# Encoder layer on one core: two of the last eight output slices scaled and stored by GpSimd, one by VectorE, six stores left to SyncE

## Chip, cores, metric

The kernel is one launch on one core of one Trainium2 chip. The metric is device time in microseconds (us), the median of three runs. The profile is of one further execution of the same program; its times count from the start of its span.

## What is computed

One encoder layer (windowed attention, a long convolution, a gated merge, a squared-ReLU MLP) runs over two groups of tokens with shared weights: 512 tokens ("sample") and 256 tokens ("prompt"). What the change touches is the very last step, the final modulated RMSNorm of the residual stream:

```
shf, scf = jnp.split(c_act @ w_ada_final + b_ada_final, 2, axis=-1)
return modulate(rmsnorm(x, final_g), shf, scf)
# rmsnorm: y = x * rsqrt(mean(x*x) + eps) * g       modulate: y * (1 + scale) + shift
```

Everything is float32, D_MODEL is 1024.

## The kernel before

The activations lie transposed in on-chip memory: 128 partitions hold the features of one of eight slices (`KD = 8`), the columns are the 768 tokens, 512 of the sample group (half 0) and 256 of the prompt group (half 1). The program is written engine by engine, each engine's instructions in the order in which its block issues them, with semaphores between engines; nothing is scheduled by a planner.

At the end of the MLP, TensorE makes the last down projection for the sixteen (half, slice) pairs in the order of `PART_ORDER`, all of half 0 first. For each, VectorE adds the result to the residual stream `xT` (`residual_group`, L2198), ScalarE squares it (L1306), and TensorE sums the squares over the partitions. When half 0 is complete its scale 1/rms is spread over a PSUM tile `wk`, and its eight slices are normalised, scaled and stored between the steps of half 1: VectorE writes `y = xT * wk` (`t_half`, L1798), ScalarE applies the per-feature scale and shift (`y_half` of the scalar block, L1344), SyncE stores the slice (L598).

Half 1, 256 tokens, comes after the last matmul and is all that is left then. After its 1/rms (ScalarE L1725, VectorE L1770, TensorE L824) VectorE runs `t_half(2, 1, k)` for k = 0 to 7. Slices 2 and 5 (`Y_DVE`) are also scaled and shifted by VectorE itself (`y_half` of the vector block, L1807), each behind the `t_half` of the next slice; slices 0, 1, 3, 4, 6, 7 by ScalarE. SyncE stores all eight in the order 0 to 7 (L607), each behind the semaphore of its producer (`y_act`, `y_dve`), and then waits until all sixteen stores have landed (`stored`). A slice of half 1 is 128 x 256 float32, 128 KB.

GpSimd works on this kernel's early parts: additions of the convolution (L644, L683 to L713) and loads of weights from its own DMA queue (L634, L732, L740). Its last instruction in the program is the last load at L740.

Of the kernel before, what the change touches and what calls it, by code (L numbers as in the profile page):

```python
# [17 lines left out]
ALU = mybir.AluOpType  # L18
# [4 lines left out]
KD = D // P  # L23
# [32 lines left out]
SH1, SC1, G1, SH2, SC2, G2, SHF, SCF = (8 * i for i in range(8))  # L56
# [34 lines left out]


PART_ORDER = [(h, m) for h in range(2) for m in range(KD)]
Y_DVE = (2, 5)


LATE_DOT = [len([n for n in range(DOTS_OUT) if n % 3 == s]) for s in range(2)]
# [9 lines left out]
def program(nc, a, out_T):  # L107
    with ExitStack() as ctx:
        def sem(name):
            return ctx.enter_context(nc.semaphore(name))  # L110

        def region(*layouts):

            def size(layout):
                total = 0
                for _, shape, _ in layout:
                    n = 1
                    for d in shape[1:]:
                        n *= d
                    total += n  # L120
                return total

            assert max(map(size, layouts)) == size(layouts[-1])
            got = []
            for layout in layouts[:-1]:
                with ExitStack() as e:
                    got.append([e.enter_context(nc.sbuf_tensor(*t)) for t in layout])
            got.append([ctx.enter_context(nc.sbuf_tensor(*t)) for t in layouts[-1]])
            return got


        def sb(name, shape, dt=F32):
            return ctx.enter_context(nc.sbuf_tensor(name, shape, dt))
# [3 lines left out]
        wlo = [sb(f"w_lo{i}", [P, KD, P], F32R) for i in range(2)]  # L137

        (sqA, accA, _, mraw_c, _, crow, mrow), (wA,), (act,) = region(
            [("n0_sq", [P, 2, T], F32), ("n0_acc", [P, T], F32), ("act_gap", [P, 3 * T], F32), ("mod_raw_c", [P, 2, 512], F32),  # L140
             ("act_gap2", [P, 8 * T - P - 1024], F32), ("c_turned", [16, P], F32), ("mod_rows", [P, 2 * T], F32)],
            [("w_down_hilo", [P, 6, 2, KD, P], F32R)],
            [("act_hilo", [P, 2, KD, T], F32R)])

        ((hfA, fa, h1, zst, zh, fb, fk, ftab, dec, dec_p, ftab_p), (_, w3l),
         (_, cb3, junk3, _, ring3, s3f, c_st),
         (cos, sin, rt, vtmp, S0, PT0, S1, PT1, _, mask, _),
# [58 lines left out]
        modT = sb("modT", [P, 64, 2])  # L206
        asc = sb("norm_scale", [P, 3, KD, 2])
# [42 lines left out]
        f_stored = [sem(f"f_stored{i}") for i in range(4)]  # L250
        asc_done = sem("asc_done")
        m_sum, m_out, sqrt_set = sem("mod_sum"), sem("mod_out"), sem("sqrt_set")
        n_sq, n_acc, n_ps, n_std, n_rstd, n_spread, n_t, n_hf, n_hi, n_lo = (
            sem(n) for n in ("n_sq", "n_acc", "n_ps", "n_std", "n_rstd", "n_spread", "n_t", "n_hf", "n_hi", "n_lo"))
# [4 lines left out]
        fwd_ready, cross_step, prod_done = sem("fwd_ready"), sem("cross_step"), sem("prod_done")  # L259
        pc_copied, rot_done, pair_step = sem("pc_copied"), sem("rot_done"), sem("pair_step")  # L260
        tap_bias = sem("tap_bias")
        spec_first = m_sum
        inv_ready, inv_copied, y_done, z_done = (sem(n) for n in ("inv_ready", "inv_copied", "y_done", "z_done"))
        s_ready, s_max, s_neg, s_sd, s_es, s_exp, s_den, s_rden, s_norm = (
# [6 lines left out]
        y_act, y_dve, stored = (sem(n) for n in ("y_act", "y_dve", "stored"))  # L271
# [101 lines left out]
        def half(h):  # L373
            return slice(GROUPS[h][0], GROUPS[h][0] + GROUPS[h][1])

        def y_out(h, m):
            return out_T[:, m, half(h)]
# [90 lines left out]
        def _(sp):  # L468
# [128 lines left out]
                sp.wait_ge(y_act, m + 1)  # L597
                sp.dma_start(y_out(0, m), yT[:, m, half(0)]).then_inc(stored, 16)  # L598
            na = nd = 0
            for m in range(KD):  # L600
                if m in Y_DVE:
                    nd += 1
                    sp.wait_ge(y_dve, nd)
                else:
                    na += 1
                    sp.wait_ge(y_act, KD + na)
                sp.dma_start(y_out(1, m), yT[:, m, half(1)]).then_inc(stored, 16)  # L607
            sp.wait_ge(stored, 16 * 2 * KD)


        @block.gpsimd
        def _(pool):
# [125 lines left out]
            for n in range(KD, DOTS - DOTS_OUT):  # L738
                pool.wait_ge(dot_done, 2 * DOTS_OUT + 2 * n)
                pool.dma_start(ring3[:], w_adaT[n + DOTS_OUT]).then_inc(ld_dot[2], 16)  # L740

# [525 lines left out]
        def _(act_e):  # L1269
# [71 lines left out]
            def y_half(h, k):  # L1341

                act_e.wait_ge(n_t, 3 * KD + KD * h + k + 1)
                act_e.activation(yT[:, k, half(h)], yT[:, k, half(h)], ACT.Identity,  # L1344
                                 bias=modT[:, SHF + k, h:h + 1], scale=asc[:, 2, k, h:h + 1]).then_inc(y_act, 1)
# [146 lines left out]
            for t in range(T_MERGE):  # L1492
# [14 lines left out]
                elif t < T_GATE:  # L1507
                    m = t - T_HY
# [218 lines left out]
                if u >= KD:  # L1727
                    y_half(0, u - KD)
            for k in range(KD):
                if k not in Y_DVE:  # L1730
                    y_half(1, k)


# [1 line left out]
        def _(dve):  # L1735
# [53 lines left out]
            def t_half(q, h, k):  # L1789

                if k == 0:
                    dve.wait_ge(n_spread, 2 * q + h)
                if k == 1 and (q, h) != (2, 1):
                    dve.wait_ge(n_acc, KD + 16 * (q - 1) + KD * h + KD)
                if k >= 2 and q == 1:
                    dve.wait_ge(n_hf, KD + KD * h + k - 1)
                dst = yT[:, k, half(h)] if q == 2 else tnB[:, k % 2, half(h)]
                dve.tensor_tensor(dst, xT[:, k, half(h)], wk[:, half(h)], ALU.mult).then_inc(n_t, 1)  # L1798
# [5 lines left out]
            def y_half(k):  # L1804

                dve.wait_ge(n_t, 4 * KD + k + 1)
                dve.tensor_scalar(yT[:, k, half(1)], yT[:, k, half(1)], asc[:, 2, k, 1:2],  # L1807
                                  modT[:, SHF + k, 1:2], ALU.mult, ALU.add).then_inc(y_dve, 1)
# [716 lines left out]
            norm_rstd(2, 1)  # L2525
            for k in range(KD):
                t_half(2, 1, k)
                if k - 1 in Y_DVE:
                    y_half(k - 1)


def tables():
# [138 lines left out]
```

## Time and profile before

| | us |
|---|---|
| median of three runs | 1113.33 |
| lowest, highest | 1111.73, 1113.34 |
| the profiled execution, its own time | 1114.14 |
| its span | 1112.6 |

| engine | busy us | share of the span |
|---|---|---|
| TensorE (PE) | 1092.2 | 98% |
| TensorE weight loads (PEld) | 1022.2 | 92% |
| VectorE (DVE) | 802.3 | 72% |
| ScalarE (ACT) | 454.5 | 41% |
| GpSimd (POOL) | 108.9 | 10% |

The execution's own time is 1.5 us above its span: that much lies around what the profile shows. SyncE only issues DMAs, and such instructions are not counted as busy; a name with q (SPq, POOLq) is an engine's instruction queue. "TENSOR_TENSOR y<-xT,wk" reads: the instruction writes tile `y` from tiles `xT` and `wk`. A time to landing runs from the issue of a DMA to its completion.

### The profile page before, as it was taken

The page shows a single profiled execution, that of the slowest core. Times are in us where ns is not written, and L with a number is a line of the kernel's source. Part 1 is how long each engine was busy: PE and PEld are TensorE (multiplying, and loading weights), DVE is VectorE, ACT ScalarE, POOL GpSimd, SP SyncE. Part 2 cuts the span into 40 slices and gives each one's busy share as a digit, 9 for nine tenths or more (in the row PEclk, how much of TensorE's full clock was granted, in tenths as well). Part 3 has the DMA queues.
Part 4 walks back from the last instruction along what each step waited for, and adds up shares of the span by engine and source line. Part 5 has one row for each costly group of instructions (what it writes and reads, how often), then busy time and mean ns, then how long its engine had stood idle before and what let it go on. Part 6 is the DMA issues. An engine that isn't in the chain of part 4 may idle for free.

```text
span 1112.6 us, 16634 instructions
## 1 busy us (share of the span) xinstructions
PE 1092.2 (98%) x6304; PEld 1022.2 (92%) x6304; DVE 802.3 (72%) x1334; ACT 454.5 (41%) x792; POOL 108.9 (10%) x132
## 2 busy tenths in 40 slices
PE   6999999999999999999999999999999999999997
PEld 4787798888899999999899999999999999999886
DVE  5777699889388685556455777787978778788534
ACT  5631156665722322423246232253442526157414
POOL 2101200000334322000000000000000000000000
PEclk9999999999999999999999999999999999999998
DMA  9923454333332333753312331143333232222303
GB/s 345 394 86 117 154 189 143 129 127 114 119 123 105 119 104 124 282 153 108 110 57 95 125 121 57 57 152 99 111 103 106 95 109 91 87 76 76 95 19 115
DMA packets 45525, 138.85 MB, mean 125 GB/s; under 512 B 5051, under 2 KB 10635, under 8 KB 44556
## 3 DMA queue, kind: packets, MB, share of 16 engines
q1 hardware_dynamic: 29024, 80.21, 21.6%
q0 software_dynamic: 11376, 44.84, 11.3%
q10 hardware_dynamic: 5052, 12.81, 3.3%
q8 instruction: 47, 0.77, 0.3%
q14 instruction: 26, 0.21, 0.1%
HBM read 121.61 MB, written 15.74 MB: 123 GB/s over the span
## 4 chain that ended last, share of the span: by engine, by line
PE 93%; DVE 4%; DMA 1%; ACT 1%; issue 0%; ACTq 0%; DVEq 0%
PE acc_ps L750 39%; PE wk L1181 16%; PE acc_ps L1200 12%; PE acc_ps L832 12%; PE wk L1056 2%; PE acc_ps L839 1%; PE wk L991 1%; PE wk L980 1%; PE wk L970 1%; PE wk L1022 1%; PE wk L872 1%; PE wk L885 1%; DVE dot_out L1832 1%; DMA filt_zh<-in_t_z 1%; PE wk L803 1%; PE wk L890 1%
## 5 line engine op out<-in xcount | busy, mean ns | idle before, releaser
L750 PE MATMUL acc_ps<-act_hilo,w_hi 128*128 128x384 f32 x1504 | 332.5, 342 | 0.1
L750 PEld LDWEIGHTS acc_ps<-act_hilo,w_hi 128*128 128x128 f32 x1504 | 264.8, 189 | 18.8 <-issue 17.7
L750 PE MATMUL acc_ps<-act_hilo,w_lo 128*128 128x384 f32 x752 | 191.5, 335 | 0.0
L750 PEld LDWEIGHTS acc_ps<-act_hilo,w_lo 128*128 128x128 f32 x752 | 136.4, 188 | 0.0
L1200 PE MATMUL acc_ps<-hidden_hilo,act_hilo 128*128 128x384 f32 x768 | 134.6, 335 | 0.2
L1200 PEld LDWEIGHTS acc_ps<-hidden_hilo,act_hilo 128*128 128x128 f32 x768 | 133.2, 188 | 1.1 <-issue 1.1
L1741 DVE TENSOR_TENSOR w_lo<-w_raw,w_hi 128x1024 fp32r<-128x1024 f32 x61 | 76.3, 1252 | 55.1 <-ACT w_hi L1282 54.1
L1282 ACT ACTIVATE w_hi<-w_raw 128x1024 fp32r<-128x1024 f32 x61 | 64.2, 1053 | 44.3 <-PE acc_ps L750 40.9
L2198 DVE SCALAR_TENSOR_TENSOR xT<-acc_ps,modT,xT 128x512 f32<-128x512 f32 (+1 forms) x32 | 19.7, 617 | 59.7 <-PE acc_ps L832 59.5
L1832 DVE CUSTOM_DVE_ANT_0 dot_out<-dot_ring,c_rows,vecT 128x1024 f32<-128x1024 f32 x48 | 61.6, 1284 | 1.6 <-issue 0.6
L2323 DVE SCALAR_TENSOR_TENSOR xT<-acc_ps,modT,xT 128x384 f32<-128x384 f32 (+2 forms) x96 | 40.5, 478 | 28.8 <-PE acc_ps L1200 28.8
L750 PE MATMUL acc_ps<-hidden_hilo,w_hi 128*128 128x384 f32 x256 | 54.7, 334 | 0.0
L1515 ACT ACTIVATE gates_out<-acc_ps 128x768 f32<-128x768 f32 x16 | 13.0, 813 | 98.3 <-PE acc_ps L750 98.3
L832 PE MATMUL acc_ps<-hidden_hilo,w_down_hilo 128*128 128x512 f32 (+1 forms) x288 | 50.2, 336 | 0.0
L832 PEld LDWEIGHTS acc_ps<-hidden_hilo,w_down_hilo 128*128 128x128 f32 x288 | 44.4, 190 | 5.6
L1181 PE MATMUL wk<-act_hilo,w_hi 128*128 128x384 f32 x192 | 48.7, 334 | 0.0
L1181 PE MATMUL wk<-t_hilo,w_hi 128*128 128x384 f32 x192 | 48.7, 334 | 0.0
L2305 DVE TENSOR_TENSOR c_st<-wk,c_st 128x384 f32<-128x384 f32 x84 | 44.9, 551 | 2.7 <-PE wk L1181 2.3
L750 PEld LDWEIGHTS acc_ps<-hidden_hilo,w_hi 128*128 128x128 f32 x256 | 45.3, 188 | 0.0
L1614 ACT ACTIVATE act_hilo<-w_raw 128x512 fp32r<-128x512 f32 x32 | 20.0, 626 | 59.0 <-PE acc_ps L1200 59.0
L2312 DVE TENSOR_TENSOR hidden_hilo<-c_st,hidden_hilo 128x384 fp32r<-128x384 f32 x48 | 26.8, 558 | 22.5 <-ACT hidden_hilo L1633 22.2
L1605 ACT ACTIVATE w_hi<-s_sum 128x512 fp32r<-128x512 f32 x24 | 14.9, 628 | 64.1 <-DVE s_sum L2280 64.1
(301 smaller groups left out, 2026.4 us busy)
## 6 DMA issues: line engine op xcount, KB each, us to landing
w_raw<-in_w_pre SPq DMA_DIRECT2D x50, 512.0 KB, 3.5
dot_ring<-in_w_ada_cols POOLq DMA_DIRECT2D x48, 512.0 KB, 3.8
w_raw<-in_w_up SPq DMA_DIRECT2D x32, 512.0 KB, 3.7
w_raw<-in_w_down SPq DMA_DIRECT2D x16, 512.0 KB, 3.4
w_raw<-in_w_down_half SPq DMA_DIRECT2D x32, 256.0 KB, 2.7
spec<-filt_out POOLq DMA_DIRECT2D x12, 512.0 KB, 2.9
gate_spill<-gates_out ACTq DMA_DIRECT2D x16, 384.0 KB, 2.3
hy_spec<-spec SPq DMA_DIRECT2D x12, 512.0 KB, 5.6
```

Source lines behind the costliest of these rows:

```text
L750: mm = pe.matmul(acc_ps[:, slot, 512 * h:512 * h + HALF], w[:, k, :], src[:, x, k, HALF * h:HALF * h + HALF], start=(first and i == 0), st ...
L832: mm = pe.matmul(acc_ps[:, slot, half(h)], w_i[:, k, :], src[:, x, k, half(h)], start=(n == 0 and i == 0), stop=(n == KD - 1 and i == 2))
L1056: mm = pe.matmul(wk[:, c + o:c + o + P], w, x, start=(i == 0), stop=(i == 1))
L1181: mm = pe.matmul(st_ps(q, j), w[:, k, :], st_act(j, x, k), start=(k == 0 and i == 0), stop=(k == PK - 1 and i == 2))
L1200: mm = pe.matmul(acc_ps[:, m % 2, 512 * h:512 * h + HALF], w[:, k, :], hid[:, x, k, HALF * h:HALF * h + HALF], start=(k == 0 and i == 0), ...
L1282: act_e.activation(whi[s][:] if to is None else to[0], raw[s][:], ACT.Copy).then_inc(hi_done, 1)
L1614: act_e.activation(st_weight(ST_DOWN[m % 3])[0], quarter(m % 4), ACT.Copy).then_inc(sd_hi, 1)
L1741: dve.tensor_tensor(lo, raw[s][:], hi, ALU.subtract).then_inc(lo_done, 1)
L1832: dve.tensor_tensor_reduce(junk[:], ring[:, i], cb[:, g], 1.0, vT[:, V_BA + mt:V_BA + mt + 1], ALU.mult, ALU.add, modT[:, mt, g:g + 1]).th ...
L2305: dve.tensor_tensor(dst, st_ps(q, j), other, ALU.add).then_inc(st_u, 1)
L2312: dve.tensor_tensor(hid_block(q, b, 1), c_block(b), hid_block(q, b, 0), ALU.subtract).then_inc(h4_lo, 1)
L2323: last = dve.scalar_tensor_tensor(xT[:, m, a:b], acc_piece(s, a, b), modT[:, G2 + m, g:g + 1], xT[:, m, a:b], ALU.mult, ALU.add)
```

## The change

The table `Y_DVE` is replaced by two: `Y_ENGINE` names the engine that scales each slice of half 1, `Y_STORE` the order of SyncE's stores. ScalarE now scales slices 0, 2, 3, 5, 6; GpSimd scales 1 and 4 and stores each from its own DMA queue, behind its own result; VectorE scales slice 7 after all eight `t_half`. SyncE stores 0, 2, 3, 5, 7, 6. GpSimd's block ends with a wait for its two stores. The semaphores `tap_bias` (under the name `y_pool`) and `f_stored[0]` are used again; both have their earlier counts (4 and 3 x 16) by then.

```
-Y_DVE = (2, 5)
+Y_ENGINE = ("act", "pool", "act", "act", "pool", "act", "act", "dve")
+Y_STORE = (0, 2, 3, 5, 7, 6)
@@ SyncE
-            for m in range(KD):
-                if m in Y_DVE:
+            for m in Y_STORE:
+                if Y_ENGINE[m] == "dve":
                     nd += 1
                     sp.wait_ge(y_dve, nd)
                 else:
                     na += 1
                     sp.wait_ge(y_act, KD + na)
                 sp.dma_start(y_out(1, m), yT[:, m, half(1)]).then_inc(stored, 16)
-            sp.wait_ge(stored, 16 * 2 * KD)
+            sp.wait_ge(stored, 16 * (KD + len(Y_STORE)))
@@ GpSimd, behind its last weight load
+            ny = 0
+            for k in range(KD):
+                if Y_ENGINE[k] == "pool":
+                    ny += 1
+                    pool.wait_ge(n_t, 4 * KD + k + 1)
+                    pool.tensor_scalar(yT[:, k, half(1)], yT[:, k, half(1)], asc[:, 2, k, 1:2],
+                                       modT[:, SHF + k, 1:2], ALU.mult, ALU.add).then_inc(y_pool, 1)
+                    pool.wait_ge(y_pool, 4 + ny)
+                    pool.dma_start(y_out(1, k), yT[:, k, half(1)]).then_inc(f_stored[0], 16)
+            pool.wait_ge(f_stored[0], 16 * (3 + ny))
@@ ScalarE
-                if k not in Y_DVE:
+                if Y_ENGINE[k] == "act":
                     y_half(1, k)
@@ VectorE
                 t_half(2, 1, k)
-                if k - 1 in Y_DVE:
-                    y_half(k - 1)
+                if Y_ENGINE[k] == "dve":
+                    y_half(k)
```

The end of VectorE's block before, from the last 1/rms on (`y` is the output tile, `wk` the spread 1/rms in PSUM):

```order
L1770 RECIPROCAL norm_rstd<-norm_rstd 128x2 [waits n_std]
L1798 TENSOR_TENSOR y<-xT,wk 128x256 [waits n_spread]
L1798 TENSOR_TENSOR y<-xT,wk 128x256 x3
L1807 TENSOR_SCALAR y<-y,norm_scale,modT 128x256 [waits n_t]
L1798 TENSOR_TENSOR y<-xT,wk 128x256 x3
L1807 TENSOR_SCALAR y<-y,norm_scale,modT 128x256 [waits n_t]
L1798 TENSOR_TENSOR y<-xT,wk 128x256
```

and now:

```order
L1782 RECIPROCAL norm_rstd<-norm_rstd 128x2 [waits n_std]
L1810 TENSOR_TENSOR y<-xT,wk 128x256 [waits n_spread]
L1810 TENSOR_TENSOR y<-xT,wk 128x256 x7
L1819 TENSOR_SCALAR y<-y,norm_scale,modT 128x256 [waits n_t]
```

The eight products stand in one row, and a single scaling stands behind them.

The end of GpSimd's block in the changed kernel (before, it ended with the sixteen loads):

```order
L739 DMA c_rows<-c_spill 128x2048 [waits acc_ready]
L742 DMA dot_ring<-in_w_ada_cols 128x1024 [waits dot_done] x16
L748 ISA
L748 TENSOR_SCALAR y<-y,norm_scale,modT 128x256 [waits n_t]
L751 DMA out_T<-y 128x256 [waits tap_bias]
```

The last two rows follow once more, for slice 4. The ISA row is a reload of GpSimd's code library that the build puts ahead of the scaling. It waits for nothing, so it stands between the last weight load and the wait of the first scaling.

## Rows read from the trace of the kernel before

**Rows 1.** The chain of waits, in order of time: start us, us, what.
```profile
1084.20 18.73 PE acc_ps L832 x156
...
1105.10 0.72 PE wk L824 x4
...
1105.85 1.41 DVE y L1798 x4
...
1108.90 0.34 DVE y L1798
1109.24 0.02 issue
1109.27 0.60 ACT y L1344
```

**Rows 2.** Timeline of SyncE's queue, stores of half 1: start us, us, instruction.
```profile
1106.93 0.33 SPq L607 DMA_DIRECT2D out_T<-y  x1
1107.42 0.33 SPq L607 DMA_DIRECT2D out_T<-y  x1
1107.80 0.45 SPq L607 DMA_DIRECT2D out_T<-y  x1
1108.29 0.45 SPq L607 DMA_DIRECT2D out_T<-y  x1
...
1110.27 0.44 SPq L607 DMA_DIRECT2D out_T<-y  x1
```

**Rows 3.** Timeline of VectorE and ScalarE over half 1.
```profile
1105.85 0.42 DVE L1798 TENSOR_TENSOR y<-xT,wk 128x256 f32<-128x256 f32 x1 [0.80 <-PE wk L824]
1106.19 0.41 DVE L1798 TENSOR_TENSOR y<-xT,wk 128x256 f32<-128x256 f32 x1
...
1107.18 0.41 DVE L1807 TENSOR_SCALAR y<-y,norm_scale,modT 128x256 f32<-128x256 f32 x1
...
1106.31 0.60 ACT L1344 ACTIVATE y<-y,modT,norm_scale 128x256 f32<-128x256 f32 x1 [0.76 <-DVE y L1798]
1106.81 0.58 ACT L1344 ACTIVATE y<-y,modT,norm_scale 128x256 f32<-128x256 f32 x1
```

**Rows 4.** Line 108, SyncE behind its stores: ns min/median/max, first to last start.
```profile
L108 SPq COMPARE_BRANCH  x1: 38/38/38, 1112.1 to 1112.1; - x1
L108 SPq EVENT_SEMAPHORE  x1: 17/17/17, 1112.6 to 1112.6; - x1
```

**Rows 5.** Busy time in half-microsecond stretches; the last two numbers are DMA share and GB/s.
```profile
1108.50:1109.00 0.50, 0.00 (x0) 0.00 (x0) 0.50 (x3) 0.44 (x2) 0.00 (x0) 0.50 0.82 270
...
1111.00:1111.50 0.50, 0.00 (x0) 0.00 (x0) 0.00 (x0) 0.00 (x0) 0.00 (x0) 0.50 0.81 270
1111.50:1112.00 0.50, 0.00 (x0) 0.00 (x0) 0.00 (x0) 0.00 (x0) 0.00 (x0) 0.50 0.28 92
```

**Rows 6.** DMA issues of the whole span: KB each, median us to landing.
```profile
spec<-filt_out POOLq DMA_DIRECT2D x12, 512.0 KB, 2.9
gate_spill<-gates_out ACTq DMA_DIRECT2D x16, 384.0 KB, 2.3
...
out_T<-y SPq DMA_DIRECT2D x8, 256.0 KB, 2.0
...
out_T<-y SPq DMA_DIRECT2D x8, 128.0 KB, 1.8
```

**Rows 7.** Timeline of GpSimd, early parts: additions and a store's issue.
```profile
69.61 1.28 POOL L644 TENSOR_TENSOR filt_taps<-filt_taps,hy_pairs 1x512 f32<-1x512 f32 x1 [22.55 <-DVE filt_taps L1944]
...
95.19 0.53 POOL L652 DMA_DIRECT2D spec<-filt_out  x1 [0.66 <-DVE filt_out L1970]
...
125.92 1.94 POOL L644 TENSOR_TENSOR filt_taps<-filt_taps,hy_pairs 1x512 f32<-1x512 f32 x1 [3.14 <-DVE filt_taps L1944]
...
281.50 1.29 POOL L684 TENSOR_TENSOR hy_pairs<-hy_xv 128x512 f32<-128x512 f32 x1
282.87 1.04 POOL L690 TENSOR_TENSOR hy_fold<-hy_pairs 128x512 f32<-128x512 f32 x1
...
331.65 3.34 POOL L709 TENSOR_TENSOR hy_y<-hy_pairs 128x512 f32<-128x512 f32 x1
```

**Rows 8.** GpSimd's library reload, VectorE's results before two additions, GpSimd's last load.
```profile
L644 POOLq MODIFY_POOL_CONFIG  x2: 37/37/37, 47.1 to 47.1; - x2
68.24 1.22 DVE L1944 TENSOR_TENSOR filt_taps<-wk,filt_decay 128x1024 f32<-128x1024 f32 x1
124.61 1.23 DVE L1944 TENSOR_TENSOR filt_taps<-wk,filt_decay_p 128x1024 f32<-128x1024 f32 x1 [0.68 <-PE wk L872]
955.69 0.53 POOL L740 DMA_DIRECT2D dot_ring<-in_w_ada_cols  x1 [18.17 <-DVE dot_sum L2335]
```

More of the change, by code:

```diff
@@ L261, in program @@
         tap_bias = sem("tap_bias")
+        y_pool = tap_bias
         spec_first = m_sum
```

## The prediction

> **What bounds the kernel now.** I began with the page's busy shares: TensorE is busy in 98% of the span, so only what lies after the last matmul can move the time unless TensorE's own work is touched, and it is not. The chain of waits shows where that is [rows 1]: the last group of matmuls leads, through the last sums, to the spread 1/rms at 1105.10 to 1105.82, and from there the chain runs over VectorE's products and a last ScalarE scaling, which ends at 1109.87. The span ends at 1112.6. The whole change lives in those last 6.8 us, 0.6% of the time.
>
> The chain's view stops at ScalarE, so I read SyncE's queue next [rows 2]. Eight stores start at 1106.93, 1107.42, 1107.80 and from there every 0.49 us to 1110.27. The last slice was ready at 1109.87, so its store waited 0.40 us **in the queue and not for data**: from the third store on SyncE is the slowest member of the tail, at 0.49 us a store. A lone issue takes 0.33 us, one behind another 0.45. The last store lands 1.8 us after its start [rows 6], at 1112.07; SyncE's branch at 1112.1 agrees, and its last semaphore at 1112.6 ends the span [rows 4]. So three things could carry the end: the producers, SyncE's issues, and the 16 DMA engines. The DMA engines are the third view [rows 5]: while SyncE issues back to back they are busy 0.81 to 0.82 at 270 GB/s. One store thus takes 0.81 x 0.49 = 0.40 us of all engines. They have some room, but not much: 19%.
>
> **The change, part by part.** The sum is made against the profiled execution: 1114.14 us, which is 0.81 above the median of the runs shown.
>
> 1. *VectorE.* Two scalings of 0.41 us leave their places between the products, which start every 0.33 us [rows 3]. The eight products run from 1105.85 without a break; the last starts at 1108.17 and ends at 1108.58, 0.65 earlier than the one at 1108.82 now. The scaling of slice 7 follows it and waits for it: 1108.60 to 1109.01.
>
> 2. *ScalarE.* Five scalings in place of six, 0.49 apart, each 0.04 behind its product (the first starts at 1106.31, the product ends at 1106.27) [rows 3]. Slice 2 runs 1106.97 to 1107.56, 3 to 1108.06, 5 to 1108.55, 6 to 1109.05.
>
> 3. *SyncE.* Six issues, at the same cost each: slice 0 at 1106.93, 2 at 1107.58, 3 at 1108.08, 5 at 1108.57, 7 at 1109.06, 6 at 1109.55. Both the producer and the queue give about these times; they are in step. The last issue stands **0.72 us earlier** than 1110.27, and by itself would land at 1111.35. The order 7 before 6 costs nothing: both are ready by 1109.05.
>
> 4. *GpSimd, the scalings.* The trace has no scaling on GpSimd. Its additions of 512 columns take 1.04 to 1.29 us undisturbed, 1.94 and once 3.34 us beside VectorE's work [rows 7]. A scaling here has 256 columns and one full operand. The lower bound is half of 1.04, 0.52; the upper one a full 512-column addition in its middling form, 1.94. I take half of 1.29, 0.65, the row nearest in kind. GpSimd starts 0.08 behind the product (an addition starts at 125.92, the product before it ends at 124.61 + 1.23), waits 0.08 for its own result (281.50 + 1.29 to 282.87), and is held 0.53 by each issue [rows 7, 8]. Slice 1: product done at 1106.60, scaling 1106.68 to 1107.33, store issued at 1107.41, free at 1107.94. Slice 4, whose product is long done: scaling to 1108.59, issue at 1108.67.
>
> 5. *GpSimd, the stores.* No GpSimd store of 128 KB is in the trace. Its 512 KB stores land in 2.9 us; the other queues' stores grow from 1.8 to 2.0 to 2.3 us over 128, 256 and 384 KB, some 0.25 us per 128 KB [rows 6]. So 2.9 - 0.75 = 2.15 us; bounds are 1.8 (as on SyncE) and 2.9. Slice 4 lands at 1110.82. In general it lands at 1109.52 + 2d, with d the length of a scaling. It is late only if d exceeds 1.2 or so. What is queued behind GpSimd's waits is nothing but its own end, and nobody else waits for it.
>
> 6. *The DMA engines.* This is where part of the 0.72 goes back. The share of 0.28 after 1111.50 is 0.17 us at 0.81, so the data of the last store end at 1111.67, 0.40 before its landing; a store's 1.8 us are then 1.0 to the start of its data, 0.40 of data and 0.40 behind them [rows 5, 6]. So data can start 1.0 us behind a SyncE issue, 1.35 behind a GpSimd issue. In a line, 0.40 each: slice 0 from 1107.93, 2 from 1108.58, 1 to 1109.38, 3 to 1109.78, 5 to 1110.18, 7 to 1110.58, 4 to 1110.98, 6 to 1111.38. With 0.40 behind, the end lands at 1111.78, **0.29 us earlier** than 1112.07. On this point the Trainium skill, "DMA: Bandwidth & Descriptors", section "Issuing engines are not separate DMA queues", says that all queues share the same 16 engines and that a second issuer saves only issue time; by it the term is 0.29 and not 0.72, and the trace before, where one queue alone fills 0.81, cannot show the sharing itself.
>
> 7. *The library reload* ahead of the first scaling. It has no wait and stands behind the load at 955.69, so 150 us before the product it serves. The reload at 47.1 was followed by the first addition at 69.61, 0.15 behind its product's end at 69.46, against 0.08 at 125.92 [rows 7, 8]. Where the load is paid when it is issued it fits into 22 us, far under 150; what is paid at the first call showed as at most 0.07 us. I put it at nothing; the cover is GpSimd's idle time from 956 to 1106. If the load were paid only when the first scaling starts, it would cost from 0.07 to 22 us.
>
> Sum: -0.29 us. 1114.14 becomes 1113.85, and the median 1113.33 becomes 1113.0. A measurement of this kernel tells a change of about 0.2%, 2.2 us, from none; the whole span from the first SyncE issue to the last landing is 5.1 us.
>
> **The rivals.**
>
> *A. The transfers don't meet.* If the two GpSimd stores fit into the 19% that the engines have free, the whole 0.72 stays: 1113.4, median 1112.6. For it: room of 0.19 in each half microsecond. Against it: two stores bring 0.80 us of work, and some 2.5 us of room hold 0.5.
>
> *B. GpSimd is the last.* With d at 1.28 slice 4 lands at 1112.08 and nothing changes; above that the change costs twice the excess. At d = 1.94 it lands at 1113.40: +1.3, median 1114.7. It would be slower by 0.2% only from d = 2.4; at the one row of 3.34, +4.1. For it: GpSimd's rows scatter upward, always with VectorE running. Against it: half the columns, and VectorE's products are over at 1108.6.
>
> *C. The code is fetched at the first call.* The reload is then not hidden, and slice 1 and all behind it on GpSimd start late by the fetch; above 1.25 us it decides. The rows bound it by 0.07 and 22 us, so the time would lie up to 21 us above now. The lag of 0.15 us speaks against it. The Trainium skill, "GPSIMD Engine Reference", section "Instruction dispatch", says that the first call to a freshly loaded kernel pays about 6 us; by its 5.95 the estimate would be slice 4 landing at 1116.8 and a median of 1118.0. The trace does not agree: 0.07 us at the first addition.
>
> *D. It doesn't do what it says.* The tail shortens, but another piece of the kernel drifts by as much, since the runs lie 1.6 us apart.
>
> **How the numbers follow.** Forecast 0.58; A 0.15; B 0.19, of which 0.02 beyond 0.2%; C 0.04; D 0.04, split over both signs. The likeliest time is 1113.0. The range takes A's 1112.6 and B's 1114.7 and, at the low end, the runs' own spread below the median, 1.6 us: 1111.2 to 1114.7. Faster by over 0.2% could only come from drift, 0.02; slower from B's far end, C and drift, 0.07; within 0.2%, 0.91.
>
> **What would show it.** SyncE's last issue near 1109.55, or 3.7 us behind the first product, instead of 4.42; GpSimd's scalings at 0.65 us, its stores landing in 2.2 us; a DMA share above 0.9 between 1109 and 1111; the last landing 5.9 us behind the first product instead of 6.2. I am wrong if a GpSimd scaling takes over 1.2 us, if its store lands after SyncE's last, or if the first scaling starts microseconds behind its product.

## The result, and the profile after

The changed kernel takes 1120.13 us (median of six runs, 1119.22 to 1121.28) against 1112.65 for the kernel before, measured in the same series (1111.21 to 1113.6). The ratio is 1.0067, 95% interval 1.0057 to 1.0078: **slower by 7.5 us**, where no change was forecast. The profiled execution took 1120.15 us with a span of 1118.5.

The span is 5.9 us longer, and the engines' work does not explain it: TensorE, VectorE and ScalarE are busy no longer than before, and GpSimd's 2.6 us more are mostly its two scalings and two issues. The chain of waits of the changed kernel, from the spread 1/rms on (start us, us, what), names the engine on which it ends:

```profile
1103.89 0.72 PE wk L836 x4
1104.62 0.02 issue
1104.64 0.76 DVE y L1810 x2
1105.40 0.10 issue
1105.50 0.56 POOL y L748
1106.07 0.29 issue
1106.35 0.60 POOL out_T L751
1106.95 0.06 issue
1107.01 0.56 POOL y L748
1107.57 0.29 issue
1107.86 0.60 POOL out_T L751
```

GpSimd has taken the place of VectorE and ScalarE [rows 1]. But its last issue is over at 1108.46, ten microseconds before the end of the span at 1118.5. What fills them is in no row of busy time. The instructions of line 109 of the changed kernel, which is the end of every engine's program (ns min/median/max, first to last start), show it:

```profile
L109 POOLq EVENT_SEMAPHORE  x2: 17/17/17, 1118.3 to 1118.4; - x2
...
L109 POOLq COMPARE_BRANCH  x1: 41/41/41, 1111.2 to 1111.2; - x1
L109 POOLq DRAIN  x1: 6917/6917/6917, 1111.3 to 1111.3; - x1
L109 SPq COMPARE_BRANCH  x1: 38/38/38, 1111.4 to 1111.4; - x1
L109 SPq DRAIN  x1: 7/7/7, 1111.6 to 1111.6; - x1
L109 SPq EVENT_SEMAPHORE  x1: 17/17/17, 1118.4 to 1118.4; - x1
```

Each engine ends with a drain, and all engines then meet at a semaphore. SyncE's drain takes 7 ns. **GpSimd's takes 6.92 us**, from 1111.3, when its stores have landed, to 1118.3. SyncE has its own stores down at 1111.4 and waits for it; the waits of its queue (us in total, times, longest) name an engine there that had long been done, so only the first number is to be read:

```profile
SPq L109 <- PEq L109: 6.9, 1, 6.9
```

The same instruction is in the kernel before, at its line 108, behind the load that the description of that kernel calls GpSimd's last instruction:

```profile
L108 POOLq DRAIN  x1: 7316/7316/7316, 955.7 to 955.7; - x1
```

There it begins while GpSimd's last weight load is being issued and is over at 963.0, 150 us before anybody needs it.

The rest of the tail, shown as SyncE's queue and GpSimd's instructions:

```profile
1104.64 2.73 DVE L1810 TENSOR_TENSOR y<-xT,wk 128x256 f32<-128x256 f32 x8 [0.80 <-PE wk L836]
1105.10 2.75 ACT L1356 ACTIVATE y<-y,modT,norm_scale 128x256 f32<-128x256 f32 x5 [0.76 <-DVE y L1810]
1105.50 0.55 POOL L748 TENSOR_SCALAR y<-y,norm_scale,modT 128x256 f32<-128x256 f32 x1 [150.50 <-DVE y L1810]
1105.72 2.97 SPq L609 DMA_DIRECT2D out_T<-y  x6
...
1107.41 0.41 DVE L1819 TENSOR_SCALAR y<-y,norm_scale,modT 128x256 f32<-128x256 f32 x1
```

Executions differ by a microsecond or so in when the matmuls end, so from here on I compare **tails**: from the start of the first product of half 1 to the end of the span. The span is read to 0.1 us, and a tail is no better than that. Before: 1105.85 to 1112.6, 6.75 us. Changed: 1104.64 to 1118.5, 13.86 us. The difference, 7.1 us, is nearly the 7.5 of the medians. SyncE's last store is issued at 1108.25, 3.61 us into the tail instead of 4.42 [rows 2], so the change does what it says. Its landing, at SyncE's branch, comes 6.76 us into the tail instead of 6.25 [rows 4]: half a microsecond **later**. So 0.5 us of the loss is in the transfers and 6.6 in the drain.

### The profile page after: what moved, and what is told of

Its sections match the earlier page's. It is cut to its first block, busy times and chain, and to the rows that moved or that the text cites. A ratio compares the mean times of both kernels' runs of the same rounds, so it can differ in the third digit from the quotient of the medians.

```text
span 1118.5 us, 16637 instructions
## 1 busy us (share of the span) xinstructions
PE 1092.0 (98%) x6304; PEld 1020.7 (91%) x6304; DVE 800.7 (72%) x1333; ACT 453.9 (41%) x791; POOL 111.5 (10%) x136
## 4 chain that ended last, share of the span: by engine, by line
PE 90%; DVE 4%; DMA 2%; issue 1%; ACT 0%; SPq 0%; POOL 0%; DVEq 0%; ACTq 0%
PE acc_ps L762 38%; PE wk L1193 16%; PE acc_ps L1212 12%; PE acc_ps L844 12%; DMA mod_raw_b<-in_w_ada_rows 2%; PE wk L1068 2%; PE acc_ps L851 1%; PE wk L1003 1%; PE wk L897 1%; PE wk L992 1%; PE wk L982 1%; PE wk L884 1%; PE wk L1034 1%; DVE dot_out L1844 1%; DMA hy_spec<-spec 1%
```

## The experiments

Three theories stood at first: (1) GpSimd's drain takes some 7 us wherever it begins; (2) only behind recent DMAs of its queue; (3) only behind code from the reloaded library.

**GpSimd scales, SyncE stores all.**

```
+Y_STORE = (0, 1, 2, 3, 4, 5, 7, 6)
@@ SyncE also waits for y_pool, ahead of slices 1 and 4
@@ GpSimd
-                    pool.wait_ge(y_pool, 4 + ny)
-                    pool.dma_start(y_out(1, k), yT[:, k, half(1)]).then_inc(f_stored[0], 16)
-            pool.wait_ge(f_stored[0], 16 * (3 + ny))
```

> The changed kernel, but SyncE stores all eight slices (order 0, 1, 2, 3, 4, 5, 7, 6); GpSimd only scales slices 1 and 4 and then ends. The tail, from the start of the first product of half 1 to the end of the span, is 6.75 us before and 13.86 in the changed kernel. Theory 1 (GpSimd's drain takes some 7 us whatever came before, and all engines wait for it): GpSimd is free at 2.4 us of the tail, the drain ends at 9.3 to 9.7, tail 9.6 to 10.0, time 3.0 us over before. Theory 2 (the drain is long only for a GpSimd queue that has lately issued DMAs): it is short, tail 6.5 to 6.8, time as before. Theory 3 (it is long after code of the reloaded library): as theory 1.

Measured: 1114.98 against 1112.27 us, ratio 1.0021 (1.0011 to 1.0031); tail 9.37. Without a late DMA the drain is still long:

```profile
1106.37 0.56 POOL L751 TENSOR_SCALAR y<-y,norm_scale,modT 128x256 f32<-128x256 f32 x1 [0.43 <-DVE y L1810]
...
L109 POOLq DRAIN  x1: 7402/7402/7402, 1106.3 to 1106.3; - x1
```

The drain's record begins with the scaling's; 6.8 us lie beyond the scaling's end. Theory 2 falls. This run is needed again below for its stores: all eight go out from SyncE's queue over 3.31 us, as before (3.34), and still the last lands 6.7 us into the tail, against 6.25 before.

**SyncE waits for GpSimd's stores.**

```
@@ GpSimd
-            pool.wait_ge(f_stored[0], 16 * (3 + ny))
@@ SyncE
             sp.wait_ge(stored, 16 * (KD + len(Y_STORE)))
+            sp.wait_ge(f_stored[0], 16 * 5)
```

> The changed kernel, but SyncE and not GpSimd waits for the landing of GpSimd's two stores, so GpSimd drains as soon as its second store is issued. Theory 1 (fixed 7 us from where it begins): the drain begins 3.85 us into the tail instead of 6.65, tail 11.0 to 11.3, 2.6 to 2.8 us less than the changed kernel. Theory 2b (the drain waits for the stores to land and then takes its 7 us): tail 13.9, no gain.

Measured: 1115.89 against 1112.27, ratio 1.0040 (1.0024 to 1.0055); tail 11.02, 2.8 less than the changed kernel. The drain's record begins with the last issue and ends 6.93 us behind that issue's end, though the store lands 3.3 us after it was issued: the drain does not wait for the landing and then start anew.

```profile
L109 POOLq DRAIN  x1: 7557/7557/7557, 1106.4 to 1106.4; - x1
```

**The kernel before, with a late wait on GpSimd and nothing else.**

```
@@ GpSimd, behind its last weight load
+            pool.wait_ge(n_t, 4 * KD + 2)
```

> The kernel before with one instruction more: GpSimd, behind its last weight load at 955 us, waits for the product of slice 1 of half 1 and does nothing with it. Theory 1 (fixed 7 us, whatever came before): the drain begins 0.85 us into the tail and takes 7, tail 8.1 to 8.5, time 1.4 to 1.8 us over before. Theory 2 (only behind recent DMAs) and theory 3 (only behind library code): the drain is short or long past, tail 6.75, time as before.

Measured: 1113.81 against 1112.27, ratio 1.0016 (1.0006 to 1.0026); tail 7.96. One wait, behind which GpSimd does no work, costs 1.2 us of tail, since it puts the drain off until 1106.0. Theory 3 falls too: no addition or scaling has run on GpSimd for over 650 us.

```profile
L108 POOLq DRAIN  x1: 6754/6754/6754, 1106.0 to 1106.0; - x1
```

**GpSimd's two slices taken from half 0.** Slices 1 and 4 of half 0 are scaled and stored by GpSimd, half 1 is as before.

```
+Y_POOL0 = (1, 4)
@@ GpSimd, behind its last weight load
+            for ny, k in enumerate(Y_POOL0):
+                pool.wait_ge(n_t, 3 * KD + k + 1)
+                pool.tensor_scalar(yT[:, k, half(0)], yT[:, k, half(0)], asc[:, 2, k, 0:1],
+                                   modT[:, SHF + k, 0:1], ALU.mult, ALU.add).then_inc(tap_bias, 1)
+                pool.wait_ge(tap_bias, 5 + ny)
+                pool.dma_start(y_out(0, k), yT[:, k, half(0)]).then_inc(f_stored[0], 16)
+            pool.wait_ge(f_stored[0], 16 * 5)
```

> The kernel before, half 1 untouched; GpSimd scales and stores slices 1 and 4 of half 0 (512 columns), which become ready over 10 us before the end. Theory 1 (the drain takes some 7 us from GpSimd's last instruction, and costs only what is left of it at the end): GpSimd's stores are down by about 1100, the drain by about 1107, before SyncE's last landing; tail 6.7 to 6.8, time as before within 0.1%. Rival (any late GpSimd DMA or reloaded code costs some 6 us at the end wherever it stands): tail 12 to 14, time 6 us over before.

Measured: 1112.89 against 1112.12, ratio 0.9999 (0.9987 to 1.0011); tail 6.59. The same kind of work, and a drain that ends at 1103.7, about when the products of half 1 begin, cost nothing.

```profile
L109 POOLq DRAIN  x1: 6917/6917/6917, 1096.8 to 1096.8; - x1
```

**Bare programs.** They hold no layer: SyncE stores constants, GpSimd does the few instructions in question. First two memsets; then one 128 KB store behind them; then one scaling with the library reload ahead of it.

```
             pool.memset(z[:], 1.0).then_inc(zset, 1)
+            pool.memset(z[:], 2.0).then_inc(zset, 1)                                        # memset, DMA
+            pool.dma_start(out_T[:, KD - 1, TS:T], z[:]).then_inc(p_stored, 16)             # DMA
+            pool.tensor_scalar(z[:], z[:], v[:, 0:1], v[:, 1:2], ALU.mult, ALU.add)   # library
```

> A bare program that leaves the layer out and writes constants: GpSimd does two memsets and nothing else, SyncE makes all stores. Theory 1 (a fixed drain): GpSimd's drain takes 6.7 to 7.6 us even here, with no DMA and no reload in the whole program. Theory 2 (DMAs of its queue) and 3 (a reloaded library), in the weaker form in which any earlier use counts: under 1 us.

> The bare program with one 128 KB store from GpSimd's queue behind the memsets, waited for. Theory 1: the drain takes the same 6.7 to 7.6 us. Theory 2: long here and short in the memset program. Theory 3: under 1 us.

> The bare program with one scaling on GpSimd (a library reload ahead of it, no DMA from its queue). Theory 1: the drain takes the same 6.7 to 7.6 us. Theory 3: long here and short in the other two. The scaling of 256 columns takes 0.55 us as in the changed kernel; how far its start lies behind the reload shows what the reload costs when nothing hides it.

The memsets, the store, the scaling, in this order (18.86, 18.43 and 18.86 us in all; of each bare program there is one execution):

```profile
L16 POOLq DRAIN  x1: 41/41/41, 3.4 to 3.4; - x1
```

```profile
L16 POOLq DRAIN  x1: 130/130/130, 5.8 to 5.8; - x1
```

```profile
L36 POOLq MODIFY_POOL_CONFIG  x2: 11/11/11, 2.8 to 2.8; - x2
L36 POOL TENSOR_SCALAR z<-z,vec_sb x1: 555/555/555, 2.9 to 2.9; 128x256 f32<-128x256 f32 x1
...
L16 POOLq DRAIN  x1: 41/41/41, 3.7 to 3.7; - x1
```

**Theory 1 falls**: here the drain takes 0.04 us. None of my three theories held, and the numbers pointed at a fourth. One DMA adds 89 ns. GpSimd's queue issues 82 DMAs in the kernel before, 84 in the changed one, and the undisturbed drains took 6.754 (82) and 6.917 us (84, twice): 82 ns for each further DMA, and 82 x 0.082 = 6.7. Theory 4: **the drain pays for every DMA of GpSimd's queue since the last drain.** Three more bare programs test it: 40 stores of 128 rows, 40 of which all but the first have one row, and 82 memsets without a DMA.

```
-                pool.dma_start(out_T[:, KD - 1, TS:T], z[:]).then_inc(p_stored, 16)
-                pool.wait_ge(p_stored, 16)
+                for n in range(40):
+                    pool.dma_start(out_T[:, KD - 1, TS:T], z[:]).then_inc(p_stored, 16)     # or [0:1, ...]
+                    pool.wait_ge(p_stored, 16 * (n + 1))
```

> The bare program with 40 stores of 128 KB, 128 rows each, from GpSimd's queue, one after the other, in place of one. Theory 4: the drain takes 0.04 + 40 x 0.082 = 3.3 us (it was 0.041 without a DMA and 0.130 with one). Theory 1 or one in which only the last DMA counts: 0.13.

> The same with 1 store of 128 rows and 39 of a single row of 1 KB. If the drain counts DMAs (theory 4): 3.3 us as with 40 large ones. If it counts rows or descriptors: 0.1 to 0.3 us.

> The bare program without any GpSimd DMA but with 82 memsets in place of two. Theory 4 (DMAs alone count): 0.041 us as before. Rival (any GpSimd instruction counts, the real kernel has some 130 to 136): 3 to 7 us.

```profile
L16 POOLq DRAIN  x1: 3322/3322/3322, 97.9 to 97.9; - x1
```

```profile
L16 POOLq DRAIN  x1: 3335/3335/3335, 80.2 to 80.2; - x1
```

```profile
L16 POOLq DRAIN  x1: 41/41/41, 32.9 to 32.9; - x1
```

3.3 us for 40 DMAs, large or small, 0.04 for 82 memsets (103.23, 85.59 and 36.72 us in all). It is the number of DMAs, neither their rows nor GpSimd's other instructions.

**The changed kernel with an early drain.** If an earlier drain takes the count off, the change can be had without its cost.

```
@@ GpSimd, behind its last weight load
+            pool.drain()
             ny = 0
```

> The changed kernel with one instruction more: a drain of GpSimd right behind its last weight load at 955 us, where the engine is idle for 150 us. Theory 4 (the drain takes some 82 ns for each DMA that GpSimd's queue has issued since the last drain: 82 DMAs and 6.75 us, 84 and 6.92, one and 0.13 in the bare program): the early drain takes 6.8 to 7.4 us and costs nothing, the last one covers two DMAs and takes 0.1 to 0.3 us; tail 7.0 to 7.2, 6.7 us less than the changed kernel and 0.2 to 0.5 over before. Theory 4b (it counts all DMAs of the program again): last drain 6.9 us, tail 13.9 as in the changed kernel. Theory 1 (a fixed length in a program of this size): 6.9 us.

Measured: 1113.05 against 1112.21, ratio 1.0005 (0.9996 to 1.0014); tail 7.13. The early drain takes its 7.3 us at 954 where nobody waits, the last one 0.2:

```profile
L743 POOLq DRAIN  x1: 7316/7316/7316, 954.0 to 954.0; - x1
```

```profile
L109 POOLq DRAIN  x1: 215/215/215, 1110.8 to 1110.8; - x1
```

One instruction gives back 6.7 of the 7.1 us of tail. What is left, 0.4, is the transfers: SyncE's last landing stands 6.8 us into the tail here as in the changed kernel.

**What the idea is worth by other means.** Four kernels spread the stores differently: ScalarE stores one slice; GpSimd stores two but scales none; ScalarE stores those two; and GpSimd stores two behind an early drain.

```
-Y_DVE = (2, 5)
+Y_DVE = (2, 7)
@@ VectorE, behind its last product
+            y_half(KD - 1)
@@ ScalarE, behind its six scalings; SyncE leaves slice 6 out
+            act_e.wait_ge(y_act, 2 * KD - len(Y_DVE))
+            act_e.dma_start(y_out(1, 6), yT[:, 6, half(1)]).then_inc(stored, 16)
```

> The kernel before with the aim of the change but without GpSimd: VectorE scales slices 2 and 7 (7 last), ScalarE scales the other six and then stores slice 6 from its own queue, SyncE stores the other seven. SyncE's last issue stands 3.93 us into the tail instead of 4.42. If only the shared transfer engines limit: tail 6.3 to 6.5 against 6.75, 0.3 us faster, under what the times can tell. Rival (a second queue stretches SyncE's landings, as in the changed kernel where one took 3.2 us against 1.8): tail 7.0 to 7.3, 0.3 to 0.5 us slower.

Measured: 1112.80 against 1112.27, ratio 1.0001 (0.9992 to 1.0010); tail 6.38, 0.37 less than before, and too little for the times.

```
@@ GpSimd (all scalings as before; SyncE leaves slices 1 and 4 out and waits for all)
+            for m, na in ((1, 2), (4, 4)):
+                pool.wait_ge(y_act, KD + na)
+                pool.dma_start(y_out(1, m), yT[:, m, half(1)]).then_inc(f_stored[0], 16)
```

> The kernel before, all scalings where they were; slices 1 and 4 of half 1 are stored from GpSimd's queue, SyncE stores the other six and waits for all. In the changed kernel SyncE's last landing took 3.2 us and 9 to 27 GB/s trickled on for 0.6 us. Theory S (the software queue's stores make one of the 16 transfer engines late): again, SyncE's last store takes 2.5 to 3.3 us with such a trickle. Theory C (only the crowding of stores): SyncE's last issue stands near 3.9 us into the tail as ScalarE's last scaling allows, crowding is less, landing 1.8 to 2.1. The drain begins at about 3.0 us into the tail, so the tail is 10.0 to 10.5 and the time 3.5 us over before by theory 1 of the drain.

Measured: 1117.00 against 1112.05, ratio 1.0040 (1.0026 to 1.0054); tail 10.68, the drain again. SyncE's last store landed in 2.0 us, without a trickle: **theory S**, by which stores of GpSimd's queue make one transfer engine late, **falls**.

```
@@ ScalarE
+                if k in (1, 4):
+                    act_e.wait_ge(y_act, KD + (2 if k == 1 else 4))
+                    act_e.dma_start(y_out(1, k), yT[:, k, half(1)]).then_inc(stored, 16)
```

> As the one with GpSimd's stores, but slices 1 and 4 are stored from ScalarE's queue, behind their own scalings. GpSimd ends at 956 us as before, its drain is hidden. Theory S: no trickle, every landing 1.7 to 2.2 us. Theory C: the same stretch as with GpSimd's stores. ScalarE is held 0.35 to 0.5 us by each issue, so its last scaling ends up to 0.5 us later than before, and the tail is 6.6 to 7.1: as before within what the times can tell.

Measured: 1113.04 against 1112.05, ratio 1.0004 (0.9995 to 1.0014); tail 6.8. No landing is over 2.1 us, but ScalarE's scalings come later, as expected.

```
@@ GpSimd, in the kernel in which it stores two slices
+            pool.drain()
             for m, na in ((1, 2), (4, 4)):
```

> The kernel before with slices 1 and 4 stored from GpSimd's queue (scalings unchanged), SyncE waiting for all, and a drain of GpSimd at 956 us. Without the early drain this kernel's tail was 10.7 us, with SyncE's last landing at 6.1. Theory 4: last drain 0.1 to 0.3 us, tail 6.3 to 6.5 against 6.75 before, 0.2 to 0.4 us faster, under what the times can tell (ratio 0.999 to 1.000). Theory 4b or 1: tail 10.7 as without it.

Measured: 1112.15 against 1112.58, ratio 0.9998 (0.9989 to 1.0007); tail 6.5, 4.2 us less than without the early drain. Of the versions in which GpSimd works on half 1 it is the best, and its time cannot be told from the kernel before. But the last drain was expected at 0.1 to 0.3 us and took 2.58:

```profile
1106.53 0.55 POOL L747 DMA_DIRECT2D out_T<-y  x1 [0.61 <-ACT y L1351]
L108 POOLq DRAIN  x1: 2578/2578/2578, 1106.5 to 1106.5; - x1
```

Here GpSimd goes into its drain without a wait for its stores; in the changed kernel it waits for them first. The second one, issued at 1106.53, lands 2.4 us later at 1109.0, and the drain is over at 1109.1. So the count of DMAs is not all of a drain: **it also lasts until the stores in flight have landed**. With 84 DMAs to pay for this did not show, because the landing fell inside the 6.9 us. It costs nothing here, since SyncE's last store lands only at 1109.6. All four versions beat the changed kernel, the one with the late drain (1.0040 against 1.0067) by the least; none beats the kernel before beyond doubt.

## Why the prediction was wrong

The forecast was 1113.0 us in a range of 1111.2 to 1114.7; 1120.13 lies outside. (The low end is not quite what its sum gives: 1.6 below 1112.6 is 1111.0, below 1113.0 it is 1111.4. Nothing hangs on it.) Step by step:

- **Step 5 failed** in the sentence "What is queued behind GpSimd's waits is nothing but its own end, and nobody else waits for it." Its own end is a drain of 6.9 us, and all engines wait for it. It was in the trace of before, as a row of the program's last line at 955.7, in a place where it cost nothing; the prediction read that line's instructions in the last microseconds only, where SyncE's stand, and took GpSimd's end for free. The term was 0 and measures 6.6 us on the end, shown by the run that adds one early drain (from 13.86 to 7.13 us of tail) and by the one that adds only a wait (+1.2).
- Steps 1 to 3 held. VectorE's eight products ran 2.73 us without a break, ScalarE's scaling as timed, and SyncE's last issue came 3.61 us into the tail against 3.70 forecast.
- Step 4 was close: 0.55 us for a scaling against 0.65, in the bare program too. The wait for its own result was 0.30 before a store, not 0.08, and the issue took 0.60, not 0.53. The second store went out 3.22 us into the tail against 2.82.
- Steps 5 and 6, the landings: GpSimd's first store took 2.3 us (2.15 forecast), its second 3.3; SyncE's last two 2.5 and 3.2 against 1.8 and some queueing. The forecast end of the transfers was 5.93 us into the tail, it came at 6.76. So this term was -0.29 and measures +0.5. The DMA share in half-microsecond stretches of the changed kernel (last two numbers: share, GB/s):

```profile
1108.50:1109.00 0.50, 0.00 (x0) 0.00 (x0) 0.00 (x0) 0.00 (x0) 0.00 (x0) 0.50 1.01 332
...
1109.50:1110.00 0.50, 0.00 (x0) 0.00 (x0) 0.00 (x0) 0.00 (x0) 0.00 (x0) 0.50 0.88 303
1110.00:1110.50 0.50, 0.00 (x0) 0.00 (x0) 0.00 (x0) 0.00 (x0) 0.00 (x0) 0.50 0.47 154
1110.50:1111.00 0.50, 0.00 (x0) 0.00 (x0) 0.00 (x0) 0.00 (x0) 0.00 (x0) 0.50 0.05 16
```

  The engines are full as forecast, share 0.88 to 1.01 against 0.81 [rows 5], but at the end 16 GB/s trickle on, about what one of the sixteen engines moves (332 / 16 = 21).

  Close issuing alone does not give this: with SyncE storing all eight slices over 3.31 us, as far apart as before, the last three landings took 2.2, 2.5 and 2.3 us instead of 1.8. Nor does GpSimd's queue: it stored nothing there, and the two kernels in which it stored without scaling (eight issues over 2.96 us), like the one in which ScalarE stored slice 6 (2.85 us), landed in at most 2.4 us.

  The four traces with a late end (the changed kernel, the same with SyncE's wait, with the early drain, and with SyncE storing all) share one other thing: a single transfer of kind "instruction" while the stores are in flight. In the DMA view of the changed kernel from 1109.5 to 1110.2, and of the one in which SyncE stores all from 1108.7 to 1109.7 (packets, MB, share of the 16 engines):

```profile
q14 instruction: 1, 0.01, 2.8%
```

```profile
q14 instruction: 1, 0.01, 4.6%
```

  That is 0.31 us and 0.73 us of one engine. In the seven other traces of the layer (the kernel before among them) no such transfer falls between the first product of half 1 and the last landing. Eleven traces of eleven agree, but no run moves this transfer and nothing else, so that it is the cause is likely and not shown, and why it comes at this time in these four kernels is open.
- Step 7 held: the reload is hidden. The changed kernel has it at 955.0, and the first scaling starts 0.10 us behind its product. Nor does it show where nothing hides it: the bare scaling starts 0.1 us behind its reload. Rival C, to which the Trainium skill's figure of 5.95 us gave a similar size ("GPSIMD Engine Reference", section "Instruction dispatch"), is not what happened, though its time of 1118.0 lies nearest of all; no run here shows a cost at a first call.
- Rival A did not happen; rival B's mechanism did not either, since GpSimd's last store landed at 1111.2, just before SyncE's at 1111.4. None of the three signs under "I am wrong if" came: the list held nothing by which the step that failed could have been seen.

That the drain's price is the number of the queue's DMAs, once they have landed, is shown by six lengths at five counts (0, 1, 40, 82, 84) and by the early drain. The smaller terms are read from profiles and are under what the times can tell.

## What to carry to other kernels

Before an engine gets work near the end of a program, read how that engine ends now: its drain, and how long before the end it stands. On GpSimd count the DMAs that its queue has issued since its last drain, 82 ns each; where the engine idles earlier, a drain there takes them off the end, and otherwise its last work must end that much before the others do. Its last drain still lasts until its last store has landed. When an idle engine is given work, its idle time before was cover for something; look over the whole span for what.

## What the runs showed of the hardware

- GpSimd's drain takes 0.041 us without DMAs and 0.082 us more for each DMA that its queue has issued, of 128 rows or of one: 0.130 (1), 3.322 and 3.335 (40), 6.754 (82), 6.917 us (84). SyncE's drain takes 0.007 us after some 200 DMAs of its own.
- A drain in mid-program resets this: 7.32 us at 954, 0.215 at the end, with two DMAs between.
- A drain lasts until the stores in flight have landed, but does not put that wait ahead of its count: with two DMAs since the last drain it took 2.58 us and ended 0.1 us behind the landing; with 84, behind stores in flight, it ended 6.93 us after the end of the last issue.
- A GpSimd scaling of 128 x 256 float32 with two per-partition operands takes 0.555 us, against 0.41 on VectorE and 0.60 on ScalarE [rows 3].
- In four traces the last of the eight stores landed 5.7 us after the first issue, against 5.2 before: three with the issues within 2.53 us, one with them within 3.31 us. In these four, and in none of the other seven of the layer, one 8 KB transfer of the instruction queue (0.31 or 0.73 us of one DMA engine) fell among the stores. That it is the cause is not shown.
